# A sparse-attention stage with its scores issued two units ahead and its mask product shared by two heads

## The chip, the cores and the metric

The program runs on one core of a Trainium2 chip. The metric is the device time of one execution in microseconds (us). Its five engines run their own instruction streams and meet at semaphores: PE (TensorE, matrix products, with its weight loads shown apart as PEld), DVE (VectorE), ACT (ScalarE), POOL (GpSimd) and SP (SyncE, which here issues the loads of weights).

## What is computed

One sequence of 256 tokens of width 1024 passes eleven stages: two mixers and two mixture-of-experts layers, a norm, and then feed-forward, pooling, feed-forward, feed-forward, NSA attention (`nsa`) and a last feed-forward. All inputs are float32. The change lies in the NSA stage alone, cut here to its part:

```
q: 16 heads of 64 in 4 groups; per group its own k_c,v_c (compressed), k_s,v_s (selected), k_w,v_w (window)
o_cmp = softmax(q_nope @ k_cmp.T * scale, mask of 15 blocks) @ v_cmp
o_sel = softmax(where(token <= query, q_rot @ k_s.T * scale, -1e30)) @ v_s
o_win = softmax(where(0 <= query - key < 256, q_rot @ k_w.T * scale, -1e30)) @ v_w
out   = (g0 * o_cmp + g1 * o_sel + g2 * o_win) @ w_o
```

With 256 tokens there are four selection blocks and all of them are picked, and the window spans the sequence, so the selected and the window branch are both plain causal attention over their own keys.

## The kernel before

The work of the two causal branches is cut into 16 units (`nsa_units`, line 428): two query tiles `t` of 128 tokens, four head groups `g`, two branches `br`, in that order, so that units 0 to 7 are of `t = 0` and see 128 keys (`nk = 1`; called short here), and units 8 to 15 are of `t = 1` and see 256 keys (`nk = 2`; long). A unit holds four heads. Its steps, and the helper that issues each:

- PE `scores(i)` (line 1124): the scores of the four heads go to the two PSUM banks `2*(i%2)` and the next, two heads to a bank, each head in 256 columns. First the causal mask is written into the columns of the diagonal block as a product of the identity with the mask table `causal_r` (line 1128, one product of 128 columns per head, four in all), then the scores are accumulated onto it (line 1132, four products of 64 rows).
- DVE `stats(i)` (line 2133): the negated maximum of each row and head, read from PSUM.
- ACT `exps(i)` (line 1564): four exponentials with their sums, from PSUM into `NB.P[i%2]`.
- DVE `scale(i)` (lines 2141, 2145, 2148): reciprocal of the sums, times the gate, times the probabilities in `NB.P`.
- PE `turn(i)` (line 1147): transposes the probabilities into PSUM banks 4 and 5.
- ACT `take(i)` (line 1570) copies bank 4, and for long units DVE `take(i)` (line 2154) copies bank 5, into `NB.PT[i%2]`.
- PE `values(i)` (line 1157): products with the values. For the second branch it also adds the compressed branch (line 1162), and ACT `take_outputs` copies the sum out.

Copies on ACT show as line 1235 and reciprocals on DVE as line 1626, where the helpers stand. Products of float32 operands show as two records each, those of the rounded type (`causal_r`, `ident_r`) and the transposes as one.

The orders are written by hand, one for each engine, and the waits are semaphore counts kept by `w.to`. Ahead of the loop PE issues `scores(0)` and `scores(1)` between the products of the compressed branch (line 1183), then `turn(0)` and the transposes of the compressed probabilities (line 1190). In its loop over i = 1 to 15 PE issues `scores(i+1)`, `turn(i)`, `values(i-1)`; DVE issues `stats(i+1)`, `scale(i)`, `take(i-1)`; ACT issues `exps(i)`, `take(i-1)` and, for every second unit, `take_outputs`. `turn(i)` waits for `scale(i)` and for both copies of unit i-1. After the loop comes the output projection (line 1207), 64 records of full-width products, and then the last feed-forward.

Of the kernel before, what the change touches and what calls it, by code (L numbers as in the profile page):

```python
# [14 lines left out]
P = 128  # L15
SEQ, D = 256, 1024
# [121 lines left out]
def build(nc, a, out, stages):  # L138
    ctx = ExitStack()
    with ctx:  # L140
        def sb(name, shape, dt=F32):
            return ctx.enter_context(nc.sbuf_tensor(name, shape, dt))
# [4 lines left out]
        PS = ctx.enter_context(nc.psum_tensor("PS", [P, 8, 512], F32))  # L147
# [22 lines left out]
        ident_r, causal_r = sb("ident_r", [P, P], F32R), sb("causal_r", [P, P], F32R)  # L170
# [42 lines left out]
        S = Fields()  # L213
# [214 lines left out]
        def nsa_units():  # L428

            u = [(t, g, br, t + 1) for t in range(TT) for g in range(4) for br in range(2)]  # L430
            return u, len(u)

        def nsa_scores(i, keys):

            return PS[:, 2 * (i % 2):2 * (i % 2) + 2, :].rearrange("p h (s k) -> p (h s) k", s=2)[:, :, 0:keys]
# [237 lines left out]
        def _(pe):  # L673
            w = Follow()
            n = [0]

            def slot():
                r = n[0] % RING
                n[0] += 1
                pe.wait_ge(S.loaded[r], w.to(S.loaded[r], 16))  # L680
                return r

            def view(r, k, width):
                return ring[:, r, 0:k * width].rearrange("p (k n) -> p k n", k=k)
# [362 lines left out]
            def nsa():  # L1047
                units, n_units = nsa_units()
# [62 lines left out]
                for j in range(16):  # L1111
                    for s_ in range(2):
                        last = pe.matmul(PS[64 * s_:64 * s_ + 60, 1, 0:256], NB.Z[s_][:, j, :], wv[s_][:, j, :],
                                         start=(j == 0), stop=(j == 15))
# [8 lines left out]

                def scores(i):
                    t, g, br, nk = units[i]
                    for h in range(2):
                        for s_ in range(2):
                            pe.matmul(PS[:, 2 * (i % 2) + h, s_ * SEQ + t * P:s_ * SEQ + (t + 1) * P], ident_r[:, :], causal_r[:, :],
                                      start=(s_ == 0), stop=False, skip_group_check=True)
                    for s_ in range(2):  # L1130
                        for h in range(2):
                            last = pe.matmul(PS[:, 2 * (i % 2) + h, s_ * SEQ:s_ * SEQ + nk * P],  # L1132
                                             NB.qrT[DH * h:DH * (h + 1), 2 * g + s_, t * P:(t + 1) * P],
                                             NB.kT[br][DH * h:DH * (h + 1), g, 0:nk * P],
                                             start=False, stop=True, skip_group_check=True)
                    last.then_inc(S.scored, 1)

                def turn(i):
                    t, g, br, nk = units[i]
                    pe.wait_ge(S.p_scaled, w.to(S.p_scaled))  # L1140
                    if i:
                        pe.wait_ge(S.turned_act, w.to(S.turned_act))
                        if units[i - 1][3] == 2:
                            pe.wait_ge(S.turned_dve, w.to(S.turned_dve))
                    for kt in range(nk):
                        for j in range(4):
                            last = pe.transpose(PS[:, 4 + kt, j * P:(j + 1) * P], NB.P[i % 2][:, j, kt * P:(kt + 1) * P], ident)  # L1147
                    last.then_inc(S.turned, 1)

                def values(i):  # L1150
                    t, g, br, nk = units[i]
                    o = 6 + (t * 4 + g) % 2
                    if br == 0 and i >= 4:
                        pe.wait_ge(S.oT_taken, w.to(S.oT_taken))
                    for kt in range(nk):
                        for h in range(2):
                            pe.matmul(PS[DH * h:DH * (h + 1), o, 0:SEQ], NB.v[br][:, kt, g * DH:(g + 1) * DH],  # L1157
                                      NB.PT[i % 2][:, kt, 2 * h:2 * h + 2, :], start=(br == 0 and kt == 0), stop=False,
                                      skip_group_check=True)
                    if br == 1:  # L1160
                        for s_ in range(2):
                            last = pe.matmul(PS[:, o, s_ * P:(s_ + 1) * P], NB.Vbd[:, g, s_, :],
                                             NB.PcT[:, t, g, :], start=False, stop=True,
                                             skip_group_check=True)
                        last.then_inc(S.oT_done, 1)
# [7 lines left out]
                for g in range(4):  # L1173
                    for c in range(2):
                        last = pe.matmul(PS[0:NCMP, 7, g * DH:(g + 1) * DH],
                                         NB.hcT[:, c, 64 + g * NCMP:64 + (g + 1) * NCMP], w2v[:, c, :],
                                         start=(c == 0), stop=(c == 1))
# [3 lines left out]
                for t in range(TT):  # L1181
                    for m in range(8):
                        last = pe.matmul(PS[:, 6 + t, m * 32:m * 32 + 2 * NCMP], NB.qnT[:, m, t * P:(t + 1) * P],
                                         NB.KC[:, m // 2, :], start=True, stop=True)
                    last.then_inc(S.cscored, 1)
                turn(0)
                for t in range(TT):
                    pe.wait_ge(S.p_ready, w.to(S.p_ready))
# [1 line left out]
                        last = pe.transpose(PS[:, 6 + t, g * P:(g + 1) * P], NB.P32[:, t, 4 * g:4 * g + 4, :].rearrange("p a b -> p (a b)"), ident)  # L1190
                    last.then_inc(S.p_turned, 1)
                for i in range(1, n_units):
                    if i + 1 < n_units:
                        scores(i + 1)
                    turn(i)
                    if i == 1:
                        pe.wait_ge(S.pT_ready, w.to(S.pT_ready, 2))
                    values(i - 1)
                pe.wait_ge(S.turned_act, w.to(S.turned_act))
                pe.wait_ge(S.turned_dve, w.to(S.turned_dve))  # L1200
                values(n_units - 1)
                wv = [view(slot(), 4, D) for _ in range(2)]
                pe.wait_ge(S.oT_taken, w.to(S.oT_taken, 2))
                for t in range(TT):
# [8 lines left out]
            for name in stages:  # L1213
                if name == "moe0":
                    pe.wait_ge(S.param_loaded, PARAMS)
                if name[:3] == "mix":
                    mixer(int(name[3]))
                elif name[:3] == "moe":
                    moe(int(name[3]))
                elif name[:3] == "ffn":  # L1220
                    ffn(name)
                elif name == "pool":
                    pool_mix()
                elif name == "nsa":
                    nsa()
# [389 lines left out]
        def _(v):  # L1615
            w = Follow(S.dve_step)
# [8 lines left out]
            def reciprocal(o, i):  # L1625
                v.reciprocal(o, i).then_inc(S.dve_step, 1)
                v.wait_ge(S.dve_step, w.to(S.dve_step))
# [437 lines left out]
            def nsa():  # L2065
                units, n_units = nsa_units()
                for b in (1, 3):
                    v.wait_ge(S.hT_psum, w.to(S.hT_psum, 2))
                    for k in range(2):
                        i = v.tensor_scalar(hT[:, 2 * b + k, :], PS[:, 4 + b, k * SEQ:(k + 1) * SEQ],  # L2070
                                            gT[:, 5, 2 * b + k:2 * b + k + 1], None, ALU.mult)
# [59 lines left out]
                def stats(i):  # L2131
                    v.wait_ge(S.scored, w.to(S.scored))
                    v.tensor_reduce(NB.stat[:, i % 4, 0:4], nsa_scores(i, units[i][3] * P), AX_X, ALU.max, negate=True) \
                        .then_inc(S.maxed, 1)
# [16 lines left out]
                def take(i):  # L2151
                    if units[i][3] == 2:
                        v.wait_ge(S.turned, w.to(S.turned))
                        v.tensor_copy(NB.PT[i % 2][:, 1, :, :].rearrange("p r q -> p (r q)"), PS[:, 5, :]) \
                            .then_inc(S.turned_dve, 1)
                    else:
                        w.past(S.turned)
# [29 lines left out]
                for t in range(TT):  # L2187
                    v.wait_ge(S.cexp, w.to(S.cexp))
                    cs = NB.cs[:, 2 + 2 * t, :]
                    fac = NB.cs[:, 3 + 2 * t, :]  # L2190
                    v.tensor_reduce(cs, NB.Sc[t], AX_X, ALU.add).then_inc(S.dve_step, 1)
                    v.wait_ge(S.dve_step, w.to(S.dve_step))
                    reciprocal(fac, cs)
                    v.scalar_tensor_tensor(fac, fac, some[:, t:t + 1], NB.gts[:, t, 0:16], ALU.mult, ALU.mult).then_inc(S.dve_step, 1)
                    v.wait_ge(S.dve_step, w.to(S.dve_step))
                    v.tensor_tensor(NB.P32[:, t, :, 0:NCMP], NB.Sc[t], fac.unsqueeze(2)
                                    .to_broadcast([P, 16, NCMP]), ALU.mult).then_inc(S.p_ready, 1)
                for i in range(1, n_units):
                    if i + 1 < n_units:
                        stats(i + 1)  # L2200
                    scale(i)
                    take(i - 1)
                take(n_units - 1)
                w.past(S.hT_psum, 0)
                first_low("ffn11")
# [55 lines left out]
```

## Time and profile before

| | |
|---|---|
| median of 3 runs | 2402.0 us (2398.58 to 2406.98) |
| the profiled execution | 2401.99 us |
| its span, first to last instruction | 2400.2 us |
| busy: PE, DVE, ACT | 2183.7, 767.0, 632.6 us |
| mean granted TensorE clock | 0.933 of 2.4 GHz |
| NSA loop, from the loop's first scores to the last output copied | 2050.5 to 2173.5 us |

The profile is of one execution on the chip. Times of rows are from the start of its span. The last row of the table is the stretch that the change touches, about a twentieth of the span. A granted clock of 1.00 is 2.4 GHz and 0.50 is 1.2 GHz.

### The profile page before, as it was taken

The page shows a single profiled execution, that of the slowest core. Times are in us where ns is not written, and L with a number is a line of the kernel's source. Part 1 is how long each engine was busy: PE and PEld are TensorE (multiplying, and loading weights), DVE is VectorE, ACT ScalarE, POOL GpSimd, SP SyncE. Part 2 cuts the span into 40 slices and gives each one's busy share as a digit, 9 for nine tenths or more (in the row PEclk, how much of TensorE's full clock was granted, in tenths as well). Part 3 has the DMA queues.
Part 4 walks back from the last instruction along what each step waited for, and adds up shares of the span by engine and source line. Part 5 has one row for each costly group of instructions (what it writes and reads, how often), then busy time and mean ns, then how long its engine had stood idle before and what let it go on. Part 6 is the DMA issues. An engine that isn't in the chain of part 4 may idle for free.

```text
span 2400.2 us, 28474 instructions
## 1 busy us (share of the span) xinstructions
PE 2183.7 (91%) x12030; PEld 1495.8 (62%) x12030; DVE 767.0 (32%) x1119; ACT 632.6 (26%) x886; POOL 35.9 (1%) x53
## 2 busy tenths in 40 slices
PE   7889999999878899999998899899999999768998
PEld 5754444444457544444444799699989955545998
DVE  1331111111013301111111655565565532334554
ACT  1221111111112111111111433433343323324333
POOL 5000000000000000000000000000000000000000
PEclk9779999999987799999999999999999999559999
DMA  9317999999952179999999742554454355002440
GB/s 288 136 70 306 422 422 422 422 422 422 408 183 97 70 315 421 423 422 422 422 422 411 259 166 96 219 194 175 172 205 164 134 187 189 23 1 105 176 141 35
DMA packets 142459, 599.18 MB, mean 250 GB/s; under 512 B 6913, under 2 KB 22337, under 8 KB 126002
## 3 DMA queue, kind: packets, MB, share of 16 engines
q1 hardware_dynamic: 139730, 592.27, 63.1%
q0 software_dynamic: 2656, 5.86, 1.0%
q8 instruction: 55, 0.90, 0.2%
q14 instruction: 18, 0.15, 0.0%
HBM read 597.06 MB, written 1.05 MB: 249 GB/s over the span
## 4 chain that ended last, share of the span: by engine, by line
PE 64%; DMA 26%; DVE 6%; ACT 2%; issue 1%; SPq 0%; DVEq 0%; ACTq 0%
DMA ring<-in_w_expert_up 25%; PE PS L972 19%; PE PS L848 11%; PE PS L986 9%; PE PS L718 3%; PE PS L1059 3%; PE PS L814 3%; PE PS L704 2%; PE PS L959 2%; PE PS L859 1%; PE PS L1207 1%; PE PS L837 1%; PE PS L1147 1%; PE PS L1157 1%; PE PS L1132 1%
## 5 line engine op out<-in xcount | busy, mean ns | idle before, releaser
L848 PE MATMUL PS<-ring,xs 128*64 128x512 f32 x2048 | 466.0, 609 | 56.0 <-DMA ring<-in_w_expert_up 54.7
L848 PEld LDWEIGHTS PS<-ring,xs 128*64 128x64 f32 x2048 | 160.6, 140 | 355.1 <-issue 352.1
L1235 ACT ACTIVATE split<-ring 128x2048 fp32r<-128x2048 f32 x132 | 253.1, 1920 | 424.2 <-PE PS L972 268.0
L1688 DVE TENSOR_TENSOR split<-ring,split 128x2048 fp32r<-128x2048 f32 x132 | 302.3, 2293 | 176.6 <-ACT split L1235 171.3
L972 PE MATMUL PS<-hT_high,split 128*128 128x256 f32 x2560 | 329.2, 281 | 0.0
L972 PEld LDWEIGHTS PS<-hT_high,split 128*128 128x128 f32 x2560 | 316.5, 189 | 2.8
L986 PE MATMUL PS<-split,ffn_hid 128*128 128x512 f32 x1056 | 246.9, 390 | 0.0
L859 PE MATMUL PS<-ring,work 128*64 128x512 f32 x1024 | 226.8, 596 | 0.0
L986 PEld LDWEIGHTS PS<-split,ffn_hid 128*128 128x128 f32 x1056 | 195.5, 188 | 38.9
L972 PE MATMUL PS<-hT_low,split 128*128 128x256 f32 x1280 | 178.4, 282 | 0.0
L1235 ACT ACTIVATE work<-PS 128x512 f32<-128x512 f32 (+1 forms) x73 | 47.4, 655 | 451.3 <-PE PS L884 325.9
L972 PEld LDWEIGHTS PS<-hT_low,split 128*128 128x128 f32 x1280 | 163.6, 189 | 0.0
L1849 DVE SCALAR_TENSOR_TENSOR y_low<-PS,work,y_high 128x1024 fp32r<-128x1024 f32 x32 | 41.1, 1283 | 353.7 <-ACT y_high L1388 353.7
L1844 DVE TENSOR_TENSOR work<-PS,work 128x512 f32<-128x512 f32 x32 | 22.1, 692 | 410.3 <-PE PS L848 410.3
L859 PEld LDWEIGHTS PS<-ring,work 128*64 128x64 f32 x1024 | 70.7, 137 | 131.7 <-issue 127.9
L837 PE MATMUL PS<-work,hp 128*128 128x128 f32 x1088 | 132.9, 283 | 3.0 <-DVE work L1826 3.0
L837 PEld LDWEIGHTS PS<-work,hp 128*128 128x128 f32 x1088 | 129.9, 199 | 3.2 <-issue 3.2
L1388 ACT ACTIVATE y_high<-PS,work 128x1024 fp32r<-128x1024 f32 x32 | 35.6, 1113 | 207.7 <-PE PS L859 207.7
L718 PE MATMUL PS<-hT,ring 128*128 128x256 f32 x384 | 83.2, 379 | 0.0
L718 PEld LDWEIGHTS PS<-hT,ring 128*128 128x128 f32 x384 | 73.1, 190 | 9.8
L1235 ACT ACTIVATE xs<-PS 128x512 f32<-128x512 f32 x68 | 40.6, 597 | 130.4 <-PE PS L837 130.4
L1059 PE MATMUL PS<-ring,hT 128*128 128x512 f32 (+1 forms) x192 | 72.9, 539 | 0.4 <-ACT hT L1496 0.4
(265 smaller groups left out, 1742.3 us busy)
## 6 DMA issues: line engine op xcount, KB each, us to landing
ring<-in_w_expert_gate SPq DMA_DIRECT2D x64, 2048.0 KB, 17.4
ring<-in_w_expert_up SPq DMA_DIRECT2D x64, 2048.0 KB, 17.7
ring<-in_w_expert_down SPq DMA_DIRECT2D x64, 2048.0 KB, 14.4
ring<-in_ffn_w_gate SPq DMA_DIRECT2D x20, 2048.0 KB, 8.4
ring<-in_ffn_w_up SPq DMA_DIRECT2D x20, 2048.0 KB, 8.9
ring<-in_ffn_w_down SPq DMA_DIRECT2D x20, 2048.0 KB, 7.9
ring<-in_w_in SPq DMA_DIRECT2D x8, 2048.0 KB, 18.7
ring<-in_nsa_w_in SPq DMA_DIRECT2D x5, 2048.0 KB, 7.8
```

The lines of the kernel that those rows point to most:

```text
L704: last = pe.matmul(PS[:, banks[t], offs[t]:offs[t] + width], hT[:, k, t * P:(t + 1) * P], wv[:, k, :], start=(k == 0), stop=(k == KT - 1))
L718: last = pe.matmul(PS[:, banks[c // 2], (c % 2) * SEQ:(c % 2 + 1) * SEQ], wv[:, k, c * P:(c + 1) * P], hT[:, k, :], start=(k == 0), stop=( ...
L814: last = pe.matmul(PS[:, 4 * part + 2 * t + h, :], src[:, c, t * P:(t + 1) * P], wv[:, c, h * 512:(h + 1) * 512], start=(c == 0), stop=(c ...
L837: last = pe.matmul(PS[:, 6 + b, (k % 4) * P:(k % 4 + 1) * P], hp[:, t, k * P:(k + 1) * P], EB.OH[:, t, :], start=(t == 0), stop=(t == 1))
L848: last = pe.matmul(PS[e * CAP:(e + 1) * CAP, bank, :], xs[:, k, e * CAP:(e + 1) * CAP], view((r + e) % RING, KT, DE)[:, k, :], start=(k == ...
L859: last = pe.matmul(PS[e * CAP:(e + 1) * CAP, 6 + c, :], EB.hT[:, k, e * CAP:(e + 1) * CAP], view((r + e) % RING, 4, D)[:, k, c * 512:(c + ...
L959: last = pe.matmul(PS[:, 2 * (kind == "up") + ft, 0:SEQ], split_cols(0, kind, part)[:, k, ft * P:(ft + 1) * P], hx[:, k, :], start=(n_ == ...
L972: last = pe.matmul(PS[:, bank, ft * SEQ:(ft + 1) * SEQ], split_cols(b, kind, part)[:, k, ft * P:(ft + 1) * P], hx[:, k, :], start=(n_ == 0 ...
L986: last = pe.matmul(PS[:, 2 * t + c, :], ffn_hid[:, b % 2, hpart, ft, t * P:(t + 1) * P], wv[:, ft, c * 512:(c + 1) * 512], start=(b == 0 a ...
L1059: last = pe.matmul(PS[:, banks[t], offs[t]:offs[t] + width], hT[:, k, t * P:(t + 1) * P], wv[:, k, :], start=(k == 0), stop=(k == KT - 1))
L1235: return act.activation(o, i, ACT.Copy)
L1688: v.tensor_tensor(at[:, 1], src, at[:, 0], ALU.subtract).then_inc(S.ffn_low, 1)
```

## The change

On PE, `scores` runs two units ahead of `turn` in place of one. Since the scores of unit i+2 go into the banks of unit i, a wait is added for the exponentials of unit i (`exped`), from the third unit on. `scores(2)` moves ahead of `turn(0)`. The mask of the two heads of a bank is written by one product: the moving operand is the mask table repeated twice by a broadcast, and its output is the two 128-column pieces of the bank. On DVE, the order in the loop becomes `take(i-1)`, `scale(i)`, `stats(i+2)`. ACT's order is the same. The counters of `exped` on PE are moved on by two at the end, since the last two units are waited for by nobody there.

```diff
                 def scores(i):
                     t, g, br, nk = units[i]
+                    if i >= 2:
+                        pe.wait_ge(S.exped, w.to(S.exped))
                     for h in range(2):
-                        for s_ in range(2):
-                            pe.matmul(PS[:, 2 * (i % 2) + h, s_ * SEQ + t * P:s_ * SEQ + (t + 1) * P], ident_r[:, :], causal_r[:, :],
-                                      start=(s_ == 0), stop=False, skip_group_check=True)
+                        two = PS[:, 2 * (i % 2) + h, :].rearrange("p (s k) -> p s k", s=2)
+                        pe.matmul(two[:, :, t * P:(t + 1) * P], ident_r[:, :],
+                                  causal_r[:, :].unsqueeze(1).to_broadcast([P, 2, P]),
+                                  start=True, stop=False, skip_group_check=True)
...
+                scores(2)
                 turn(0)
...
                 for i in range(1, n_units):
-                    if i + 1 < n_units:
-                        scores(i + 1)
+                    if i + 2 < n_units:
+                        scores(i + 2)
                     turn(i)
...
+                w.past(S.exped, 2)
...
+                stats(2)
                 for i in range(1, n_units):
-                    if i + 1 < n_units:
-                        stats(i + 1)
+                    take(i - 1)
                     scale(i)
-                    take(i - 1)
+                    if i + 2 < n_units:
+                        stats(i + 2)
```

The changed file is five lines longer ahead of the loop's rows, so that line 1128 becomes 1130, 1132 becomes 1135, 1147 becomes 1150, 1157 becomes 1160, 1162 becomes 1165, and on DVE 2133 becomes 2138, 2148 becomes 2153, 2154 becomes 2159.

On PE around the start of the loop the instructions stood in this order before (line 1128 is the mask, 1132 the scores, 1183 the compressed scores, 1147 the transposes of the probabilities, 1190 those of the compressed ones, 1157 and 1162 the value products):

```order
L1183 MATMUL PS<-work 128x30 x16
L1147 MATMUL PS<-cst,work 128x128 x4
L1190 MATMUL PS<-cst,work 128x128 x8
L1128 MATMUL PS<-causal_r,ident_r 128x128 x4
L1132 MATMUL PS<-work 128x128 x4
L1147 MATMUL PS<-cst,work 128x128 x4
L1157 MATMUL PS<-work 64x256 x2
```

and with the change in this one:

```order
L1186 MATMUL PS<-work 128x30 x16
L1130 MATMUL PS<-causal_r,ident_r 128x2x128 x2
L1135 MATMUL PS<-work 128x128 x4
L1150 MATMUL PS<-cst,work 128x128 x4
L1194 MATMUL PS<-cst,work 128x128 x8
L1130 MATMUL PS<-causal_r,ident_r 128x2x128 x2
L1135 MATMUL PS<-work 128x128 x4
L1150 MATMUL PS<-cst,work 128x128 x4
L1160 MATMUL PS<-work 64x256 x2
```

The scores of unit 2 now stand ahead of the transposes of unit 0, those of unit 3 ahead of the transposes of unit 1, and each set has two mask products in place of four.

On DVE, in the long units, the order before was (line 2133 is the maximum, 1626, 2145 and 2148 the scaling, 2154 the copy of bank 5):

```order
L2154 COPY work<-PS 128x512
L2133 TENSOR_REDUCE work<-PS 128x4
L1626 RECIPROCAL work<-work 128x4
L2145 TENSOR_TENSOR work<-work 128x4
L2148 TENSOR_TENSOR work<-work 128x1024
L2154 COPY work<-PS 128x512
```

and with the change:

```order
L2159 COPY work<-PS 128x512
L1631 RECIPROCAL work<-work 128x4
L2150 TENSOR_TENSOR work<-work 128x4
L2153 TENSOR_TENSOR work<-work 128x1024
L2138 TENSOR_REDUCE work<-PS 128x4
L2159 COPY work<-PS 128x512
```

The maximum has moved from ahead of the scaling to behind it, and it is that of the unit after the next.

## Rows read from the trace of the kernel before

**Rows 1.** The page's 40 equal slices of the span: granted TensorE clock in tenths.

```profile
PEclk9779999999987799999999999999999999559999
```

**Rows 2.** Two stretches of the NSA loop: length, busy us, granted clock, DMA share, GB/s.

```profile
2050.50:2092.00 41.50, 30.71 (x146) 21.02 (x144) 9.76 (x24) 14.35 (x58) 0.00 (x0) 0.54 0.00 0
2092.00:2173.20 81.20, 54.51 (x245) 36.39 (x244) 27.49 (x43) 22.46 (x78) 0.00 (x0) 0.56 0.00 0
```

**Rows 3.** Groups of the loop, shapes apart: busy, mean ns, idle before and its releasers.

```profile
L1147 PE MATMUL PS<-cst,work 128*128 128x128 f32 x92 | 22.1, 409 | 37.3 <-DVE work L2154 21.4 <-DVE work L2148 16.0
...
L2133 DVE TENSOR_REDUCE work<-PS 128x4 f32<-128x1024 f32 x8 | 9.8, 1225 | 53.4 <-PE PS L1132 53.4
```

**Rows 4.** Chain that ended last, a long unit at 1.2 GHz: start us, us, what.

```profile
2112.92 1.94 PE PS L1147 x8
2114.86 1.91 PE PS L1157 x8
2116.76 1.05 PE PS L1128 x4
2117.81 2.03 PE PS L1132 x8
2119.87 1.23 DVE work L2133
...
2121.41 1.22 DVE work L2148
2122.63 0.61 DVE work L2154
```

**Rows 5.** The same chain, a short unit at 1.2 GHz.

```profile
2054.59 1.12 PE PS L1147 x4
2055.70 1.05 PE PS L1157 x4
...
2057.81 1.18 PE PS L1132 x8
...
2060.02 0.70 DVE work L2148
```

**Rows 6.** Groups of the loop on ACT, shapes apart, as in rows 3.

```profile
L1564 ACT ACTIVATE work<-PS,work 128x256 f32<-128x256 f32 x32 | 14.7, 472 | 33.9 <-DVE work L2133 33.9
L1235 ACT ACTIVATE work<-PS 128x512 f32<-128x512 f32 x16 | 9.6, 597 | 20.5 <-PE PS L1147 19.8 <-PE PS L1190 0.7
L1564 ACT ACTIVATE work<-PS,work 128x128 f32<-128x128 f32 x24 | 8.5, 365 | 16.0 <-DVE work L2133 16.0
L1235 ACT ACTIVATE hT<-PS 128x256 f32<-128x256 f32 x8 | 3.1, 384 | 15.8 <-PE PS L1162 15.8
```

**Rows 7.** Chain that ended last, pieces at 2.4 GHz, two stages.

```profile
2077.77 0.67 PE PS L1132 x8
...
2128.91 1.09 PE PS L1132 x8
...
2169.55 0.91 PE PS L1147 x8
2170.46 1.96 PE PS L1157 x16
2172.42 0.66 PE PS L1162 x4
...
2218.46 11.39 PE PS L972 x96
```

**Rows 8.** PE, in order of time, ahead of the loop: start us, us, [idle before].

```profile
2047.14 1.12 PE L1147 MATMUL PS<-cst,work 128*128 128x128 f32 x4 [2.58 <-DVE work L2148]
```

**Rows 9.** Stretches of unbroken PE work and one after, columns as in rows 2.

```profile
2123.40:2128.40 5.00, 5.00 (x22) 3.54 (x23) 0.00 (x0) 0.60 (x1) 0.00 (x0) 0.50 0.01 3
2128.53:2131.90 3.37, 1.44 (x11) 0.93 (x10) 1.81 (x4) 0.89 (x4) 0.00 (x0) 1.00 0.01 2
...
2112.90:2119.80 6.90, 6.88 (x28) 4.45 (x28) 0.00 (x0) 0.60 (x1) 0.00 (x0) 0.50 0.00 1
```

**Rows 10.** Chain that ended last, the last products ahead of 2128.53.

```profile
2127.23 1.15 PE PS L1162 x4
```

## The prediction

> **What bounds the kernel now.** I start with the granted clock over the whole span [rows 1]. Each slice is 60 us. Two slices near the end stand at 5, half the full 2.4 GHz, and they are those of the NSA loop. The table by stretches [rows 2] shows the same loop closer: 122.7 us in all, PE busy for 30.71 + 54.51 = 85.2 of them, DVE for 37.3, ACT for 36.8, and no transfer at all. So no engine is full, nothing comes from memory, and PE runs mostly at 1.2 GHz.
>
> Next I ask what PE waits for. By the groups [rows 3] PE is idle for 37.3 us ahead of its transposes, all of it put down to DVE, and DVE is idle for 53.4 us ahead of its long maxima, all of it put down to PE. Two engines that wait for each other are one chain, and the chain of waits shows it: in a long unit [rows 4] the scores of the next unit end (2119.84), DVE takes their maximum (1.23), then scales the unit that is due (1.22 and some 0.3 before it), then copies bank 5 (0.61), and only then PE starts the transposes (1.94), values (1.91), mask (1.05) and scores (2.03). One long unit of this kind takes 2123.38 - 2112.92 = 10.5 us, of which DVE has 3.5 with PE idle. A short one takes 2060.76 - 2054.59 = 6.2 us [rows 5], and 7 with the compressed product (line 1162). The maximum stands in this chain by order alone: it belongs to the unit after the one that is scaled.
>
> **Part one, two units ahead and the maximum last.** PE has no longer to wait for DVE within a unit. While PE does `values(i-1)`, `scores(i+2)`, DVE can copy bank 5 of unit i-1 and scale unit i, and the maximum is taken while PE transposes. Is there enough PE work to hide it? In a long unit at 1.2 GHz, PE has 1.91 of values plus the mask and 2.03 of scores between two sets of transposes [rows 4], above 4 us, against 0.61 + 0.3 + 1.22 = 2.1 us of DVE. It is enough. If the clock doubles the cover is about 0.98 + 0.33 + 0.24 + 1.09 = 2.6 us, still above 2.1. The added wait for `exped` is queued ahead of the scores, and `turn` and `values` stand behind it. The exponentials of unit i need a maximum taken a whole unit earlier, so I cost it at nothing. The cover is ACT's slack: a long unit asks of ACT 4 x 0.472 + 0.597 + half of 0.384 = 2.7 us, a short one 4 x 0.365 + 0.597 + 0.19 = 2.2 us [rows 6]. If that cover went, the exponentials of a long unit, 1.9 us, would come onto the path. What is late next is PE itself.
>
> **Part two, the mask.** Four products of 128 columns take 1.05 us at 1.2 GHz [rows 4], 0.262 each. Two products of 256 columns of the rounded type replace them. The nearest row is the feed-forward's, 11.39 / 96 = 0.119 us each at 2.4 GHz [rows 7], so 0.24 for the two and 0.47 at half clock. The bounds are 0.24 (that row) and 0.53 at 2.4 GHz (no gain, half of the old 1.05). I take 0.24, since type and width are the same. Sixteen units at the other bound would cost 16 x 0.29 = 4.6 us more.
>
> **Ahead of the loop.** `scores(2)` moves in front of `turn(0)`. PE is idle for 2.58 us there [rows 8], and mask and scores take about 0.5 + 1.18 at half clock, so it is hidden. If not, the loop starts up to 1.7 us later.
>
> **The PE sum.** With PE unbroken the loop is the sum of its products. At 1.2 GHz [rows 4, 5, 10] a short unit is 0.5 + 1.18 + 1.12 + 1.05 + half of 1.15 = 4.4 us, a long one 0.5 + 2.03 + 1.94 + 1.91 + 0.58 = 7.0. At 2.4 GHz [rows 7] a short one is 0.24 + 0.67 + 0.66 (four transposes, taken as the four records of line 1162) + 0.49 (a quarter of 1.96) + 0.33 = 2.4, a long one 0.24 + 1.09 + 0.91 + 0.98 + 0.33 = 3.55. At 2.4 GHz DVE's 2.1 + 1.23 = 3.4 us per long unit and ACT's 2.2 per short one are nearly as long, so I add for meetings at semaphores and take 2.5 and 3.7.
>
> **Which clock?** This is worth more than all the rest. In the loop before, the clock rose four times (near 2077, 2128, 2149 and 2169.5), each time at the end of an unbroken run of transposes and value products. One of them is the run of 5.00 us to 2128.4 [rows 9] that ended with line 1162 [rows 10]. It fell again at once, in a stretch where PE was busy for 1.44 of 3.37 us [rows 9]. But the unbroken 6.9 us from 2112.9 did not raise it [rows 9], and this run holds the four narrow mask products [rows 4]. The change takes away the waits that let it fall, and it makes half as many mask products, twice as wide. I take it that the clock rises some 5 us into the loop and stays. Those 5 us at half speed cost 2.5 us.
>
> The sum at 2.4 GHz: 7 short units x 2.5 + 8 long x 3.7 = 47.1; two long sets of scores issued already in short units 0.8; the last values and their copy, behind the last transposes, 2.1; the start at half clock 2.5. That is 52.5 us against 122.7, a gain of 70. The output projection behind the loop is unbroken PE work whose weights are loaded, as no transfer runs in the loop, so the gain carries through to the end. The profiled execution took 2401.99 us (span 2400.2 and 1.8 around it), the median is 2402.0, so one sum serves both: 2332 us.
>
> **Rivals.**
> - *The clock rises only in the long units.* Short units hold more narrow products. Then seven short units take 4.4 in place of 2.5, less the 2.5 us already counted: 11 us more, 2343.
> - *PE is unbroken but the clock stays at 1.2 GHz.* Then 7 x 4.4 + 8 x 7.0 = 86.8, and with the edges (1.6 of early scores, 4 at the end, less 5 for the two units without scores) about 87.5: a gain of 35, 2367. For it: the run of 6.9 us without a rise [rows 9], and transposes make 1.94 of every long unit's 7.0 us at half clock. Against it: each long unit now has more of what stood ahead of the rises and less of the mask. The Trainium skill, "TensorE: Matmul & The Clock Gate", Part 4 (PE-mode transpose), says that the full clock does not engage for transposes, which would speak for this rival; the rise near 2149 came after 1.9 us of transposes and 3.1 of other products, so the trace shows no more than that a share of them does not prevent it.
> - *The look-ahead collapses: slower.* If `exped` came late, PE would sit at the new wait with `turn` and `values` queued behind it, and a unit would run one step after another: at half clock, scores and mask 2.5, maximum 1.23, exponentials 1.9, scaling 1.5, transposes 1.94, values 2.5, in all 11.6 against 10.5 in a long unit, and some 1 more in a short one as well. That is 15 us, 2417. It decides from the point where ACT's work in a unit, with its own waits, is longer than PE's; 2.7 against 3.55 or 7.0 says it isn't.
> - *The change brings only the mask.* If something else that I don't see holds PE per unit (the copies of PT, say), the idle 37.3 us stay and only 16 x 0.5 = 8 us are gained: 2394. Copies of unit i-1 are due a whole set of values and scores before `turn(i)`, which speaks against it.
>
> **How the numbers follow.** The rise early in the loop 0.62 (2332), only in the long units 0.14 (2343), never or not lastingly 0.18 (2367), only the mask 0.03 (2394), the collapse 0.03 (2417). The likeliest case alone spans 2325 (the pure PE sum without my allowance) to 2342 (a dearer mask, 4.6 us, a hidden step that isn't, 1.7, and later meetings). With the second it holds 0.76, so the range has to reach to the third: 2325 to 2368. A measurement of this kernel tells 0.3%, 7 us, from no change. Every case but the last is faster by more: faster 0.96, same 0.01, slower 0.03.
>
> **What would show it.** Right: slices or stretches of the loop at a granted clock near 1.00 except its first microseconds; a loop of 50 to 56 us; PE busy for over 90% of it; PE's idle time ahead of the transposes down from 37.3 us to under 5; no wait above 0.3 us at the mask product; two mask products per unit with starts about 0.12 us apart at 2.4 GHz; the maxima waiting for PE in DVE's own slack. Wrong in the clock: a loop of 85 to 90 us with 0.50 throughout and PE still over 90% busy. Wrong in the order: PE idle ahead of the mask product with ACT named as releaser, or ahead of the transposes with DVE still named for several us per unit. Wrong altogether: the loop is shortened and a later stage is longer by as much.

## The result and the profile after

| | before | changed |
|---|---|---|
| median, us | 2400.29 (4 runs) | 2327.96 (4 runs, 2325.88 to 2333.45) |
| ratio of the times | | 0.9701, 95% interval 0.9679 to 0.9723 |
| profiled execution, its span | 2401.99, 2400.2 | 2328.93, 2327.1 |
| mean granted clock | 0.933 | 0.953 |
| stage: start of the products of line 1113 to start of the output projection | 149.4 | 75.3 |

The change makes the kernel 3.0% faster, 72 us by the medians. The last row is used for all comparisons below. The same work ahead of the stage ends up to 10 us earlier or later from one execution to the next (the products of line 1113 start between 2019.9 and 2030.1 us in the traces of this study), so a difference of a few us shows in the stage and not in the whole time. The stage lost 74.2 us and the span 73.1.

The stage has a scatter of its own, by the moment at which TensorE's clock falls ahead of the loop. The narrow products of the compressed scores (line 1183 before, 1186 and 1185 in other kernels) show it. Below are the kernel before, the changed one, the one with DVE's order alone (the same instructions on PE as before) and the one with four mask products (the same order on PE as the changed one):

```profile
2038.59 5.97 PE L1183 MATMUL PS<-work 128*128 128x30 f32 x32 [1.02 <-DVE work L2167]
2039.03 4.20 PE L1186 MATMUL PS<-work 128*128 128x30 f32 x32 [1.18 <-DVE work L2172]
2039.92 4.18 PE L1183 MATMUL PS<-work 128*128 128x30 f32 x32 [1.02 <-DVE work L2167]
2040.20 5.96 PE L1185 MATMUL PS<-work 128*128 128x30 f32 x32 [1.02 <-DVE work L2171]
```

They take 4.2 us where the clock fell 17.4 or 17.6 us into the stage, and 6.0 where it fell 15.6 us into it, and that does not go with the kernel. So 1.8 of the 74.2 us are chance, and a difference of under 2 us between two stages shows nothing by itself.

The page's clock row of the changed kernel answers to [rows 1]. A slice is now 58 us, and no slice of the NSA loop stands at 5 any more:

```profile
PEclk9879999999989789999999899989999999999999
```

The table by stretches of the changed kernel, as in [rows 2] (length, then busy us of PE, PEld, DVE, ACT and POOL, granted clock, DMA share, GB/s), from the end of the transposes of line 1194 to the copy of the last output, and one stretch behind the stage:

```profile
2049.55:2052.40 2.85, 2.85 (x16) 2.07 (x17) 1.58 (x5) 2.17 (x10) 0.00 (x0) 0.50 0.00 0
2052.40:2090.90 38.50, 38.30 (x288) 25.31 (x285) 30.44 (x54) 29.61 (x117) 0.00 (x0) 1.00 0.00 1
2090.90:2099.90 9.00, 6.48 (x50) 4.29 (x48) 4.23 (x7) 3.45 (x13) 0.00 (x0) 1.00 0.00 0
2130.90:2134.30 3.40, 3.40 (x16) 3.23 (x17) 2.26 (x6) 2.70 (x7) 0.00 (x0) 0.50 1.05 403
```

In the first three stretches together PE is busy for 47.6 of 50.35 us, against 84.8 of the 122.6 us between the same two points before. Both things that the prediction named have happened. The waits are nearly gone and the clock is up from 2052.4 on, so PE's busy time fell by 37 us and its idle time by 35. The groups of the loop, shapes apart, answer to [rows 3]: PE's idle time ahead of the transposes fell from 37.3 us to 2.3.

```profile
L1150 PE MATMUL PS<-cst,work 128*128 128x128 f32 x92 | 13.8, 288 | 2.3 <-DVE work L2153 2.3
L2138 DVE TENSOR_REDUCE work<-PS 128x4 f32<-128x1024 f32 x8 | 9.8, 1223 | 3.4 <-PE PS L1135 3.4
```

The chain of waits shows long units in the middle of the loop, to be held against [rows 4]. They are PE alone:

```profile
2073.87 1.02 PE PS L1150 x8
2074.89 1.01 PE PS L1160 x8
2075.90 0.43 PE PS L1130 x2
2076.34 1.06 PE PS L1135 x8
2077.40 1.02 PE PS L1150 x8
2078.43 1.01 PE PS L1160 x8
2079.44 0.64 PE PS L1165 x4
...
2081.38 1.02 PE PS L1150 x8
```

From one set of transposes to the next it is 3.53 us without the compressed product and 3.98 with it, 3.76 on average, where a unit took 10.5 before. The end of the loop is a chain of DVE again, since no more PE work is left to cover it:

```profile
2087.84 1.09 PE PS L1135 x8
...
2088.95 1.22 DVE work L2138
2090.17 0.60 DVE work L2159
...
2091.08 1.24 DVE work L2153
...
2092.36 1.11 PE PS L1150 x8
```

### The profile page after: what moved, and what is told of

Same layout as the page of the kernel before. It is cut to its first block, busy times and chain, and to the rows that moved or that the text cites. A ratio compares the mean times of both kernels' runs of the same rounds, so it can differ in the third digit from the quotient of the medians.

```text
span 2327.1 us, 28410 instructions
## 1 busy us (share of the span) xinstructions
PE 2145.3 (92%) x11998; PEld 1469.0 (63%) x11998; DVE 767.1 (33%) x1119; ACT 630.8 (27%) x886; POOL 35.9 (2%) x53
## 3 DMA queue, kind: packets, MB, share of 16 engines
HBM read 597.06 MB, written 1.05 MB: 257 GB/s over the span
## 4 chain that ended last, share of the span: by engine, by line
PE 65%; DMA 27%; DVE 5%; ACT 2%; issue 1%; SPq 0%; DVEq 0%; ACTq 0%
DMA ring<-in_w_expert_up 26%; PE PS L972 20%; PE PS L848 12%; PE PS L986 10%; PE PS L718 4%; PE PS L1059 3%; PE PS L814 3%; PE PS L959 2%; PE PS L704 2%; PE PS L859 1%; PE PS L1212 1%; PE PS L837 1%; PE PS L754 1%; DMA ring<-in_w_in 1%; PE PS L731 1%
## 5 line engine op out<-in xcount | busy, mean ns | idle before, releaser
L1393 ACT ACTIVATE y_high<-PS,work 128x1024 fp32r<-128x1024 f32 x32 | 35.6, 1113 | 207.7 <-PE PS L859 207.7
## 6 DMA issues: line engine op xcount, KB each, us to landing
ring<-in_w_expert_gate SPq DMA_DIRECT2D x64, 2048.0 KB, 17.4
```

## The experiments

Theory A: the maximum ahead of the scaling tied PE and DVE into one chain. Untied, PE runs unbroken, and that by itself also raises the clock. Against it stand that the look-ahead is what counts, that the width of the mask products decides over the clock (theory B of the first experiment), and that the clock plays no part. Stages are of one profiled execution each. Times are medians, ratios are to the kernel before, timed on the same chip.

### Four mask products again

The changed kernel with the loop over `s_` back in its mask:

```diff
-                        two = PS[:, 2 * (i % 2) + h, :].rearrange("p (s k) -> p s k", s=2)
-                        pe.matmul(two[:, :, t * P:(t + 1) * P], ident_r[:, :],
-                                  causal_r[:, :].unsqueeze(1).to_broadcast([P, 2, P]), start=True, ...
+                        for s_ in range(2):
+                            pe.matmul(PS[:, 2 * (i % 2) + h, s_ * SEQ + t * P:s_ * SEQ + (t + 1) * P], ident_r[:, :], causal_r[:, :],
+                                      start=(s_ == 0), ...
```

> The changed kernel with its mask again as four products of 128 columns per unit (four in place of two). Theory A (unbroken PE work raises the clock, the merged mask only saves its own time): the loop still runs near granted clock 1.00 from some 5 us in, and loses only the mask's time, at 2.4 GHz about 0.53 against the 0.24 to 0.43 seen for the pair, so 16 x 0.2 = 3 us: 2331. Theory B (the narrow mask products were what kept the clock down in the unbroken 6.9 us stretches before): the clock stays at 0.50 for much or all of the loop and the time is 2350 to 2368.

Measured: 2334.48 us, ratio 0.972 (0.968 to 0.9759), stage 79.0 us. The clock rose at 2055.1 and stayed, and PE was as unbroken as with two products:

```profile
2055.10:2095.00 39.90, 39.85 (x310) 28.04 (x310) 30.30 (x55) 29.25 (x115) 0.00 (x0) 1.00 0.01 1
```

So theory B falls: four narrow products in a unit do not keep the clock down once PE is unbroken. The chain gives the mask's price at 2.4 GHz, for the same two places of a unit as above:

```profile
2076.53 0.40 PE PS L1130 x4
...
2080.02 0.59 PE PS L1130 x4
```

That is 0.40 against 0.24 us behind line 1165's products and 0.59 against 0.43 behind line 1160's. The mask's part of the change is 0.16 us a unit, some 2.1 us over the 13 sets of the loop. The stage is 3.7 us longer; 1.8 of these are the products of line 1185 ahead of the loop, 5.96 us against 4.20, where the clock fell earlier. That leaves 1.9 for the loop, near the mask's 2.1.

### DVE's order alone

The kernel before, one edit on DVE:

```diff
                 for i in range(1, n_units):
-                    if i + 1 < n_units:
-                        stats(i + 1)
-                    scale(i)
                     take(i - 1)
+                    scale(i)
+                    if i + 1 < n_units:
+                        stats(i + 1)
```

> The kernel before with one edit, DVE's loop order take(i-1), scale(i), stats(i+1); scores one unit ahead, four mask products. Theory A (the maximum standing ahead of the scaling was the whole tie): the wait of the transposes for DVE shrinks. At 2.4 GHz a long unit is then held by scores end, maximum 1.2, exponentials 1.9, scaling 1.5 and waits, 4.9 us, over two units with 3.95 of PE: 4.4 per unit against 3.6 in the changed kernel; a short one 3.1 against 2.6. With the mask that is 13 us behind the changed kernel: 2341, clock near 1.00. Rival (without the second unit ahead PE keeps breaking off and the clock stays at 0.50): PE-bound at half clock, 7.5 and 5.0 us per unit, about 2372. Rival (the look-ahead is what counts, the order is nothing): 2400, as before.

Measured: 2348.43 us, ratio 0.9778 (0.9736 to 0.982), stage 94.4 us. The order of three calls on DVE, with nothing changed on PE, brings 55.0 of the stage's 74.2 us. Both rivals fall. The time is 7 us over the 2341 expected. The edit moves two calls: the maximum goes behind the scaling, and the copy of bank 5 ahead of it. They were not tried apart; in the chain before [rows 4] the maximum held 1.23 us and the copy 0.61. The stage is 15.4 us behind the kernel with the second unit ahead and the same four masks, and 17.2 if the products of line 1183 and 1185 (4.18 and 5.96 us) are left out of account. The chain says where these are:

```profile
2096.18 1.94 ACT work L1564 x8
...
2098.14 0.19 DVE work L1626
...
2098.35 0.17 DVE work L2145
...
2098.55 1.22 DVE work L2148
2099.77 1.15 DVE work L2133
...
2100.94 1.94 ACT work L1564 x8
```

With one unit ahead the exponentials of unit i+1 wait for a maximum that stands behind the scaling of unit i, which waits for the exponentials of unit i. ACT and DVE close a loop of 2100.94 - 2096.18 = 4.76 us per long unit, without PE in it. I had expected 4.4. The second unit ahead breaks that loop: the maximum behind `scale(i)` is then that of i+2, and the exponentials of i+1 do not wait for it. Some 1.9 of the 17.2 us are the set of scores(2), which then moves out of the loop into PE's idle time ahead of it (0.75 us of masks and 1.18 of scores at half clock in the kernel before). PE is left with short gaps here, and the clock fell twice inside the loop, at 2080.6 and 2114.8:

```profile
2060.20:2080.60 20.40, 16.06 (x129) 11.19 (x130) 10.60 (x22) 11.10 (x49) 0.00 (x0) 1.00 0.00 1
2080.60:2087.40 6.80, 6.80 (x30) 4.81 (x30) 3.56 (x6) 3.38 (x13) 0.00 (x0) 0.50 0.00 0
2087.50:2114.80 27.30, 21.90 (x166) 15.12 (x163) 18.99 (x29) 14.47 (x55) 0.00 (x0) 1.00 0.01 2
```

### Two units ahead with the old order

The changed kernel with DVE's loop as `stats(i+2)`, `scale(i)`, `take(i-1)`:

```diff
-                    take(i - 1)
-                    scale(i)
                     if i + 2 < n_units:
                         stats(i + 2)
+                    scale(i)
+                    take(i - 1)
```

> The changed kernel with one edit, DVE's loop order as before: stats(i+2), scale(i), take(i-1); scores two ahead and the merged mask stay. Theory A (the order is the tie): scores, maximum, scaling, transposes are in one chain again, only the mask is cheaper: 16 x 0.5 = 8 us less than before, 2392, granted clock near 0.5 in the loop, PE idle some 3.5 us in each long unit. Rival (the look-ahead alone frees PE): 2330 to 2345.

Measured: 2388.09 us, ratio 0.995 (0.9934 to 0.9966), stage 132.5 us. The chain is the old one, DVE's 3.6 us and all:

```profile
2118.13 1.22 DVE work L2138
...
2119.67 1.22 DVE work L2153
2120.89 0.61 DVE work L2159
2121.50 0.14 issue
2121.64 1.94 PE PS L1150 x8
```

The look-ahead without the order is worth little against the 74, as expected. The stage is shorter by 17 us, more than the 8 I gave it; 2 of these are line 1186's products (3.93 us).

### The mask alone

The kernel before with the merged mask product, its diff as in the change:

> The kernel before with one edit, the merged mask product. Measured by the stage (start of the products of line 1113 to the start of the output projection: 149.4 us before, 132.5 in the run with scores two ahead and the old DVE order). Theory A (two ahead with the old order adds nothing of its own; what that run gained is the mask, and the more frequent spells at 2.4 GHz that come with fewer narrow products): 130 to 135 us here too, spells of granted clock 1.00 in many units, time about 2388. Theory B (two ahead gives something itself and the mask only its own time, 0.3 us in each unit on the path): 144 to 145 us, time 2396.

Measured: 2392.5 us, ratio 0.996 (0.9946 to 0.9974), stage 143.5 us. That is the side of the expectation that it calls theory B. The mask gives 6 us of the stage, and more in the loop, since in this run the clock was at half for the first products of line 1113 as well, which then took 8.81 us against 7.12. In both this run and the one before it the clock had more short spells at 2.4 GHz than in the kernel before (eight here inside the loop, where there were three; the last rise, which stayed, is not counted). One of them falls nearly whole into PE's wait for DVE:

```profile
2112.30:2119.00 6.70, 6.07 (x26) 4.03 (x26) 0.49 (x1) 0.91 (x3) 0.00 (x0) 0.50 0.00 1
2119.20:2122.50 3.30, 0.17 (x2) 0.00 (x0) 3.02 (x5) 1.82 (x8) 0.00 (x0) 1.00 0.00 0
```

A spell that falls into PE's idle time is worth nothing. The 11 us of stage between this run and the one with two units ahead are one profiled execution each; 3.7 of them lie in the products of lines 1113 and 1183 to 1186, by the clock's moment, and the intervals of the two ratios overlap. What part of the rest belongs to the look-ahead stays open.

### The gaps filled, order as before

The kernel before with products added ahead of each wait for the scaling, from unit 2 on. They multiply the identity with itself into columns 256 to 511 of bank 6 or 7, which nobody reads. The wait for `oT_taken` moves from `values` ahead of them.

```diff
+                def fill(i, n):
+                    t, g, br, nk = units[i - 1]
+                    if br == 0 and i - 1 >= 4:
+                        pe.wait_ge(S.oT_taken, w.to(S.oT_taken))
+                    for k in range(n):
+                        pe.matmul(PS[:, 6 + (t * 4 + g) % 2, SEQ:2 * SEQ], ident_r[:, :],
+                                  ident_r[:, :].unsqueeze(1).to_broadcast([P, 2, P]),
+                                  start=False, stop=False, skip_group_check=True)
...
+                    if i >= 2:
+                        fill(i, 8 if nk == 1 else 14)
                     pe.wait_ge(S.p_scaled, w.to(S.p_scaled))
```

> The kernel before, order and masks as they were, with PE's wait ahead of each transposition (from unit 2 on) filled by products of the identity with itself into columns that nobody reads: 8 of 256 columns in short units, 14 in long ones. They add work and no result changes. Theory A (half of the gain is the clock, and the clock follows unbroken PE work): the clock rises within 10 us and stays, PE's own work in the chain halves, the DVE part stays: about 4.4 per short unit and 7.4 per long one against 6.6 and 10.5, a gain of 35 to 45 us, 2355 to 2365. Rival (the clock does not answer to such work, or PE's speed is not what the units wait for): 2400 or, where the products stand in the way, up to 2410.

Measured: 2377.43 us, ratio 0.9891 (0.985 to 0.9933), stage 120.5 us, 29.0 less than before. 160 more products on PE make the kernel faster. The clock rose later than expected, with PE busy for 16.81 of 21.60 us until then, and then stayed through all of the loop:

```profile
2048.00:2069.60 21.60, 16.81 (x75) 12.86 (x76) 8.34 (x23) 8.19 (x31) 0.00 (x0) 0.50 0.08 29
2069.60:2150.00 80.40, 65.40 (x499) 50.04 (x497) 33.92 (x59) 31.80 (x116) 0.00 (x0) 1.00 0.00 1
```

A long unit took 2119.83 - 2112.09 = 7.7 us with the compressed product and 7.3 without it (expected 7.4). So the clock alone is worth 3 us of a long unit's 10.5 while the chain is as it was. It is a real part of the gain, as theory A says, and the gain is smaller than expected (2377 against 2355 to 2365), as the rise was late and fewer units had it.

### Order alone, with the gaps filled

The run with DVE's order alone and the same filling, 3 products in short and 6 in long units:

```diff
+                    if i >= 2:
+                        fill(i, 3 if nk == 1 else 6)
                     pe.wait_ge(S.p_scaled, w.to(S.p_scaled))
```

> The run with DVE's order alone (stage 94.4 us, the clock fell twice inside its loop), with 3 or 6 products of the identity added ahead of each set of transposes from unit 2 on, so that PE's gaps are shorter. Theory A (part of what that run lost against the changed kernel is clock): no fall inside the loop once it is up, stage 86 to 90 us. Rival (it is all the chain scores, maximum, exponentials, scaling of a unit one ahead, and clock plays no part): 94 to 96 us.

Measured: 2344.98 us, ratio 0.9759 (0.9737 to 0.9782), stage 89.3 us. The clock rose at 2053.4 and did not fall in the loop:

```profile
2053.40:2105.00 51.60, 50.03 (x379) 36.30 (x378) 31.43 (x57) 30.39 (x123) 0.00 (x0) 1.00 0.00 1
```

So about 5 of the 15.4 us (17.2 without the products ahead of the loop) between order alone and two units ahead are clock. The others go with the loop of ACT and DVE, which is seen best in the run before it, where PE has gaps and a long unit takes 4.76 us at full clock. It is still there at 4.77 us per long unit (2092.77 - 2088.00):

```profile
2088.00 1.94 ACT work L1573 x8
...
2090.37 1.23 DVE work L2157
2091.60 1.14 DVE work L2142
...
2092.77 1.94 ACT work L1573 x8
```

Here the filling makes PE's own work in a long unit nearly as long (3.9 us with four masks, and 0.8 of filling), so this run by itself does not tell which of the two sets the pace.

### Both copies on ACT

The changed kernel with bank 5 copied by ACT behind bank 4, to load the engine that the new wait depends on:

```diff
                     copy(NB.PT[i % 2][:, 0, :, :]..., PS[:, 4, :]).then_inc(S.turned_act, 1)
+                    if units[i][3] == 2:
+                        copy(NB.PT[i % 2][:, 1, :, :]..., PS[:, 5, :]).then_inc(S.turned_dve, 1)
```

with DVE's `take` reduced to its counter.

> The changed kernel with the copy of bank 5 moved from DVE to ACT. It tests how much slack ACT has behind the new wait for the exponentials: ACT's sum for a long unit goes from 2.8 to 3.4 us, PE's is 3.6. Theory A (PE is the bound in the loop, ACT and DVE are beside it): stage within 1.5 us of the changed kernel's 75.3. Rival (the new wait is close to deciding): PE idle ahead of the mask product or of the transposes with ACT as releaser, several us in all, stage 78 to 84.

Measured: 2330.21 us, ratio 0.9701 (0.9677 to 0.9724), stage 76.1 us, 0.8 more than the changed kernel. All of that and more is line 1186 again (5.82 us against 4.20); the loop behind it is 0.8 us shorter. PE stayed full with 0.6 us more on ACT in each long unit:

```profile
2054.50:2092.00 37.50, 37.30 (x282) 24.88 (x280) 26.37 (x46) 31.20 (x119) 0.00 (x0) 1.00 0.00 1
```

The wait for `exped` did not come to decide.

### Filling ahead of the loop

The changed kernel with products of the identity into bank 5, which is free until unit 8:

```diff
                 scores(1)
+                keep(12)
                 pe.wait_ge(S.kc_ready, w.to(S.kc_ready))
...
                 scores(2)
+                keep(10)
                 turn(0)
                 for t in range(TT):
+                    keep(3)
                     pe.wait_ge(S.p_ready, w.to(S.p_ready))
```

> The changed kernel with products of the identity (12, 10, 3 and 3, into columns nobody reads) in PE's gaps ahead of the loop, where the clock fell at 2042 and rose again at 2052.4. If the clock holds through, the 128x30 products (4.2 us) take about 2.1 and the transposes and first scores up to 2052 lose 2 more: stage 71 to 72 us against 75.3, time some 4 us (0.2%) less than the changed kernel's. If the narrow 128x30 products let it fall all the same: 75 to 77 us.

Measured: 2326.14 us (5 runs, 2322.21 to 2329.89), ratio 0.9687 (0.967 to 0.9705), stage 73.4 us. The clock fell all the same, at 2038.9, behind the narrow products, but rose 3.4 us later, ahead of the loop and not inside it:

```profile
2033.30:2038.90 5.60, 5.60 (x53) 5.39 (x51) 3.38 (x8) 0.40 (x1) 0.00 (x0) 1.00 1.06 396
2038.90:2042.30 3.40, 3.40 (x19) 3.35 (x16) 3.12 (x11) 1.80 (x9) 0.00 (x0) 0.50 0.16 55
2042.30:2093.30 51.00, 48.12 (x365) 32.44 (x364) 38.34 (x70) 36.44 (x139) 0.00 (x0) 1.00 0.00 1
```

The stage is 1.8 us shorter, half of what I had hoped for and no more than the scatter that the clock's fall gives it. The intervals of the two ratios overlap for the greater part, so over the whole kernel a gain against the changed one is not shown.

## Why the prediction was right

- **The tie.** Right. PE's wait ahead of the transposes went from 37.3 to 2.3 us. The order alone gave 55.0 of 74.2 us, and the look-ahead with the old order little. What the copy's move gave of it, apart from the maximum's, is not shown.
- **The second unit ahead.** I gave it no price of its own and argued from PE's cover for DVE. What it really does is break the loop of exponentials, scaling and maximum between ACT and DVE. It is worth 15 to 17 us behind the new order, about a third of it by the clock.
- **The mask.** The step that failed in size. I took 0.24 us for the pair, from the feed-forward's row. From its first start to the first start of the scores it takes 0.41 us behind line 1165 and 0.43 behind line 1160. (The chain counts from one modelled end to the next and shows 0.24 and 0.43: behind line 1165 it puts the difference down to that line's products, 0.64 us for four whose addition makes a unit only 0.45 longer, 3.98 against 3.53.) By the chain, with six sets at 0.43 at full clock, the loop has 1.1 us more than the sum had. The saving at half clock was 0.3 us a unit (1.05 to 0.73, or 0.75 to 0.43), not the 0.5 of the rival that brings only the mask.
- **The unit.** Taken 3.7 per long unit, measured 3.76; taken 2.5 per short one, measured 2.47 (from 2053.97 to 2056.66 and 2058.91). But the reason was another, so the match is in part luck. PE waits for next to nothing in the middle of the loop (0.20 us once, at 2070.25). The allowance for meetings was used up by the mask and, in a long unit, by the transposes, at 1.02 us where one row had given 0.91, in a short one by the values, at 0.58 where a quarter of 1.96 had given 0.49.
- **The clock.** Right in its direction and a little slow: it rose 2.85 us into the loop and stayed. The rival with the clock at 1.2 GHz fell, and so did the argument for it, that narrow mask products hold the clock down: with four of them it rose as well. Why the unbroken 6.9 us of the kernel before [rows 9] did not raise it stays open. Transposes are 1.02 of each 3.76 us and the clock held. No run here has transposes alone, so what the Trainium skill says of them, that the full clock does not engage ("TensorE: Matmul & The Clock Gate", Part 4), is not tested in itself. In this loop, where they have that share, the full clock was granted from 2052.4 on. A loop with the new order and the clock held at 1.2 GHz was not tried, so the 35 us priced for it stay an estimate.
- **Ahead of the loop.** `scores(2)` was hidden, as said. The stage also lost 1.9 us there (74.2 less the 72.3 of the loop): the clock fell later, at 2042.2 and not at 2039.8, in the middle of the narrow products of line 1186. That is not the change's doing, as the rows of these products in other runs show.
- **The loop.** 52.5 us said, 50.35 measured, and that it is so near owes something to errors that cancel. The sum takes mask and scores in all 15 units, but the last two have none: 2.7 us too many (2 x (0.24 + 1.09)), which the rival at 1.2 GHz did take off. The start at half clock lasted 2.85 us and cost 1.4, not 2.5. Against these stand 2.1 us of waits for DVE at the end of the loop (1.43 and 0.67 at line 1150) that the sum did not name.
- **Behind the stage.** The gain carried through but for 0.5 us (the stage started 0.6 us later and lost 74.2, the span lost 73.1). The last feed-forward's first products had 3.4 us at half clock, at 2130.9.
- **The slower rival.** It did not come about, and 0.6 us more on ACT in a long unit opened no gap on PE either.

## What to carry to other kernels

When two engines each show long waits for the other and neither is full, look for an instruction that stands in the shared chain by order alone, and move it behind the one that is due; it costs nothing and here it was three quarters of the gain. Then count the loops between the other engines: one unit of look-ahead may leave one closed that two units open. Work out the result at both levels of TensorE's clock, since waits inside a unit cost twice, once as idle time and once as a slower engine for the work between them.

## What was not expected of the hardware

- A price per product from a long group is too low for a short one. The feed-forward's 96 products of 128x256 take 0.119 us each [rows 7]. The two of the mask take 0.41 us, or 0.43, from their first start to the scores' first start, wherever they stand:

```profile
2079.84 0.48 PE L1130 MATMUL PS<-causal_r,ident_r 128*128 128x256 f32 x2
2080.25 1.13 PE L1135 MATMUL PS<-work 64*128 64x256 f32 x8
...
2083.35 0.50 PE L1130 MATMUL PS<-causal_r,ident_r 128*128 128x256 f32 x2
2083.78 1.13 PE L1135 MATMUL PS<-work 64*128 64x256 f32 x8
```

  The first pair stands behind line 1165, the second behind line 1160. One more product in a group of this kind costs 0.12 us again: in the run with the order alone and the gaps filled, three filling products show 0.62 us and six 0.98. So the 0.17 to 0.19 us above 0.24 come once per group. What the engine does in them was not tested.
- Work without any use made a kernel faster. Products of the identity in PE's gaps took 24 us off the kernel before (2401.15 to 2377.43).
